# Where the sample's key-query products and the final row scaling are computed in the projection stage

## The reference, cut to what matters

```python
# sample, each of the strided branches, over the cache and the new keys
scores = jnp.einsum('bthd,btnhd->bthn', q, kg) * (dh ** -0.5)
...
mixed = jnp.concatenate([o_a, o_b, o_c], axis=-1)
y = x + mixed @ w_out
...
def rmsnorm(x, g):          # the final norm, over D_MODEL = 1024
    y = xf * lax.rsqrt(jnp.mean(xf * xf, axis=-1, keepdims=True) + RMS_EPS)
    return y * g
```

## Time and profile before

| what | us |
|---|---|
| median of three runs | 1598.43 |
| lowest, highest | 1595.06, 1598.65 |
| profiled execution, its own time | 1597.11 |
| its span, first to last instruction | 1595.4 |

### The profile page before, as it was taken

How to read it: one execution, slowest core, us unless ns; L and a number is a source line. 1 busy time by engine, 2 the same in 40 slices (tenths; PEclk the granted TensorE clock), 3 DMA queues, 4 the chain that set the end, 5 groups by cost and what they waited for, 6 DMA issues and landing times. The chain is left out here.

```text
span 1595.4 us, 40264 instructions
## 1 busy us (share of the span) xinstructions
PE 1525.6 (96%) x16281; PEld 1328.2 (83%) x16281; DVE 973.1 (61%) x2108; ACT 848.5 (53%) x1633; POOL 554.9 (35%) x664
## 2 busy tenths in 40 slices
PE   7999999999999999999999998899999889999997
PEld 6998889999898989989898987886777567777775
DVE  4437766433377878788777773336666666465642
ACT  5437777322376666778888882545777511211210
POOL 1102221200155655566565542215664411121110
PEclk9999999999999999999999999997999999999999
DMA  6310112135413122121212112559990476766641
GB/s 242 103 54 30 35 43 68 57 104 145 118 38 80 49 69 63 41 77 39 69 35 68 31 46 63 149 131 218 269 207 15 152 230 197 228 218 209 216 151 40
DMA packets 196294, 175.39 MB, mean 110 GB/s; under 512 B 84915, under 2 KB 180686, under 8 KB 193806
## 3 DMA queue, kind: packets, MB, share of 16 engines
q1 hardware_dynamic: 196110, 172.82, 37.7%
HBM read 123.18 MB, written 52.84 MB: 110 GB/s over the span
## 5 line engine op out<-in xcount | busy, mean ns | idle before, releaser
L49 PE MATMUL f_bank<-c_ht,c_whi 128*128 128x384 f32 (+1 forms) x864 | 310.3, 359 | 0.5
L50 PE MATMUL f_bank<-c_ht,c_whi 128*128 128x384 f32 (+1 forms) x864 | 301.2, 349 | 1.1 <-issue 1.1
L51 PE MATMUL f_bank<-c_ht,c_wlo 128*128 128x384 f32 (+1 forms) x864 | 301.4, 349 | 0.7 <-issue 0.7
L633 POOL TENSOR_TENSOR f_scr<-f_scr 128x192 f32<-128x192 f32 (+1 forms) x180 | 113.2, 629 | 209.8 <-PE f_tps L1294 207.5
L49 PEld LDWEIGHTS f_bank<-c_ht,c_whi 128*128 128x128 f32 x864 | 162.1, 188 | 15.7 <-DVE c_wlo L929 3.0
L50 PEld LDWEIGHTS f_bank<-c_ht,c_whi 128*128 128x128 f32 x864 | 162.2, 188 | 11.5 <-issue 2.7
L51 PEld LDWEIGHTS f_bank<-c_ht,c_wlo 128*128 128x128 f32 x864 | 162.2, 188 | 8.7
L49 PE MATMUL a_s<-a_whi,a_mhi 128*128 128x512 f32 (+1 forms) x306 | 124.7, 407 | 4.8 <-DVE a_y L2533 4.8
L50 PE MATMUL a_s<-a_wlo,a_mhi 128*128 128x512 f32 (+1 forms) x306 | 121.2, 396 | 0.0
L878 ACT ACTIVATE f_scr<-f_scr 128x384 f32<-128x384 f32 (+1 forms) x180 | 92.2, 537 | 38.7 <-POOL f_scr L634 38.4
L1088 DVE COPY_PREDICATED f_scr<-f_scr,f_tps 128x384 f32<-128x384 int32 (+1 forms) x150 | 94.5, 630 | 22.8 <-PE f_tps L1294 7.5
(11 more groups left out here) (405 smaller groups left out, 3850.4 us busy)
## 6 DMA issues: line engine op xcount, KB each, us to landing
f_wraw<-in_w_in SPq DMA_DIRECT2D x27, 512.0 KB, 4.1
zs<-f_stage SPq DMA_DIRECT2D x48, 192.0 KB, 2.4
a_k<-in_ck SPq DMA_DIRECT2D x48, 192.0 KB, 5.2
a_v<-in_cv SPq DMA_DIRECT2D x48, 192.0 KB
f_scr<-in_xp SPq DMA_DIRECT2D x16, 512.0 KB, 4.4
a_x<-in_xp SPq DMA_DIRECT2D x16, 512.0 KB, 5.4
out_y_prompt<-a_y SPq DMA_DIRECT2D x16, 512.0 KB, 3.4
zt<-f_stage SPq DMA_DIRECT2D x38, 192.0 KB, 1.8
```

What stands on the lines that cost most here:

```text
L49: nc.tensor.matmul(out, w_hi, m_hi, start=start, stop=False)
L50: nc.tensor.matmul(out, w_hi, m_lo, start=False, stop=False)
L51: return nc.tensor.matmul(out, w_lo, m_hi, start=False, stop=stop)
L633: G.tensor_tensor(d[:, :, hs:], b[:, :, hs:], r, ALU.subtract)
```

## The change

Two pieces of work change their engine; their places in the list stay. The key-query product `sr` goes from GpSimd to VectorE. The operation of `ph` on VectorE is taken apart: ScalarE multiplies the tile's rows by the row factor, and GpSimd then multiplies them by `gfin`. A new semaphore, `rowed`, stands between the two.

```diff
-                elif kind == "sr":                                  # GpSimd
-                    pool.wait_ge(Z["k_in"], BASE + KLOADS * (n + 1))
-                    read(pool, "Q", n)
-                    G.tensor_tensor(kk[:, 0:FJ, :], kk[:, 0:FJ, :], qrep[:].unsqueeze(1).to_broadcast([P, FJ, AW]),
-                                    ALU.mult).then_inc(Z["product"], 1)
+                elif kind == "ph":                                  # GpSimd
+                    p, w = n % 2, rows_of(n)
+                    if n == 0:
+                        pool.wait_ge(Z["g_in"], BASE + 16)
+                    pool.wait_ge(Z["rowed"], BASE + n + 1)
+                    G.tensor_tensor(yy[p][:w, :], yy[p][:w, :], gfin[:w, :], ALU.mult).then_inc(Z["final"], 1)
...
+                elif kind == "ph":                                  # ScalarE
+                    p, w = n % 2, rows_of(n)
+                    act.wait_ge(Z["rstd"], BASE + n + 1)
+                    A(yy[p][:w, :], yy[p][:w, :], ACT.Copy, scale=small[p][:w, 2:3]).then_inc(Z["rowed"], 1)
...
+                elif kind == "sr":                                  # VectorE
+                    dve.wait_ge(Z["k_in"], BASE + KLOADS * (n + 1))
+                    read(dve, "Q", n)
+                    V.tensor_tensor(kk[:, 0:FJ, :], kk[:, 0:FJ, :], qrep[:].unsqueeze(1).to_broadcast([P, FJ, AW]),
+                                    ALU.mult).then_inc(Z["product"], 1)
...
-                elif kind == "ph":                                  # VectorE
-                    p, w = n % 2, rows_of(n)
-                    if n == 0:
-                        dve.wait_ge(Z["g_in"], BASE + 16)
-                    dve.wait_ge(Z["rstd"], BASE + n + 1)
-                    V.scalar_tensor_tensor(out=yy[p][:w, :], in0=yy[p][:w, :], scalar=small[p][:w, 2:3], in1=gfin[:w, :],
-                                           op0=ALU.mult, op1=ALU.mult).then_inc(Z["final"], 1)
```

More of the change, by code:

```diff
@@ L1839, in attend_project @@
                                         "p_far_t", "p_near", "p_far", "o_sum", "o_row", "o_back", "out", "held", "w_hi", "w_lo",
-                                        "turned", "copied", "hi", "lo", "y_sum", "resid", "square", "mean", "rstd", "final")}
+                                        "turned", "copied", "hi", "lo", "y_sum", "resid", "square", "mean", "rstd", "rowed", "final")}
         KLOADS, VLOADS = 16 * (FJ + 1), 16 * (FJ + 2)
```

## The result

The changed kernel takes 1622.55 us (median of four runs, 1619.96 to 1624.53) where the kernel before, run beside it, takes 1597.29: a ratio of 1.0151, interval 1.0132 to 1.0169, or 25.3 us more. The direction was forecast, the size not: 1614, with an upper bound of 1621.

The account below looks back on a forecast made before the run. TensorE was taken to bound the projection, other engines counting only where it waits. Places 1.6 + 9.2, clock 4.0 and tail 2.2 sum to 17.0 us on 1597.1, giving 1614; eight-in-ten range 1604 to 1621.

Parts of the forecast that it names:

- The port: VectorE beside GpSimd: GpSimd's product of 1024 elements starts 0.37 us ahead of the split and holds it, +2.31 us.
- the case in which the casts wait: The split's casts also wait for GpSimd's product: it begins 3.54 us after the power instead of 1.23, +2.31.
- GpSimd's product and ScalarE's scaling: Output rows after the power: scaling 1.06 us, product of 1024 elements 2.28; the end is 3.54 us after the power.
- The five places: TensorE's waits for `far_rows`: b = 0 pays 1.6 us; b = 2, 4, 5 and 7 pay 2.31 each, 9.2.
- tile 0's stall: VectorE's `ph` of tile 0, slowed beside GpSimd's key product; its going shortens TensorE's 4.75 us wait by 2.7.
- The key product costs nothing: On VectorE, eight times 2.55 us, in idle stretches or in place of the stall; cost nothing.
- The tail: After the last tile's power, scaling and product end at 1592.96 instead of 1590.74: +2.2 us before the store.
- The clock: TensorE's clock falls twice more, behind b = 5's longer wait and b = 0's new one: 2.0 us each, 4.0.
- The price of 1.4 to 1.5: Work in us that TensorE loses at its lower clock after one wait: 1.5 after 4.8 us, 1.4 after 1.70.
- The bound of 9: Upper bound of the clock loss in us: each of the five waits longer by about 2; the lower bound was 0.
- More is late: Rival: groups b = 1, 3 and 6 lose their 1.1 us, or the clock stays low longer: 1620 to 1625, chance 0.08.

## Why the prediction was right and where it was wrong

- *The port.* Right. The trace of before had no cast of these forms beside a GpSimd operation; the prediction took the case in which the casts wait, and 15 first casts take 2304 ns on average for 551. This agrees with what the Trainium skill, SBUF — State Buffer, section "Who interferes with whom", says of casts. The runs show what is held and for how long; that a port holds it they don't show.
- *GpSimd's product and ScalarE's scaling.* 2.28 and 1.06 us were taken, 2.39 and 1.15 measured: the right rows were chosen, each 0.1 short. The Trainium skill, GPSIMD Engine Reference, section 3.1, gives 4497 ns for 2048 columns, half of which is 2.25, an estimate that lies 0.14 under the measured 2.39.
- *The five places.* Right: 10.8 us forecast, 10.6 measured in the waits. b = 2, 4, 5 and 7 wait 15.4 us for 6.3, where 9.2 more were forecast. At b = 0 the gain from tile 0's stall and the loss met as described.
- *The key product costs nothing.* Right at seven groups (no idle time before it, 2544 ns, alone 0.9998). At b = 0 it takes back what the lost stall would give, as was said.
- *The tail.* Right: 2.2 forecast, 2.3 measured.
- *The clock.* This step failed. 4.0 us were taken, two new falls of 2.0 each, and 11.3 were lost: the term was mis-sized by 7.3, more than the 5.9 by which the 17.0 fell short of 22.9 (the small sizes above and the 0.8 us of an earlier start go the other way). Two things were wrong in it. The new falls, at b = 0 and 5, cost 3.3 us each (half of 6.52 and of 6.70 busy us). And the three places that had a stretch already were given nothing more, while b = 2 lost 3.0 us more than before and b = 7 1.6; only b = 4 stayed as it was. The price of 1.4 to 1.5 was read behind one wait of 1.70 and one of 4.75 us (for the first the window ends ahead of the stretch, so it was 1.6). As the two were alike, nothing in them said that waits of 3.6 to 4.0 would cost more. The row that would have warned is the one at b = 4, which the prediction doesn't use: behind 1.61 us of wait it has a stretch of 6.6 us, against 3.2 at its neighbours. The bound of 9 in that part ("each of the five longer by about 2") was nearer the truth than the value chosen, and with it the sum is 22.0. But even that was too low, and the range stopped at 1621. That the waits set off most of the lost clock is shown by the runs with added matmuls; what decides the length of a single stretch stays open.
- *More is late* had this case at 0.08 and 1620 to 1625. Its second half, a clock that stays low longer, was the outcome; the waits of b = 1, 3 and 6, its first half, did not come.

What stays open besides: the profiled execution is the fastest of the changed kernel's four, and its others are up to 4.6 us longer. They have no trace, so where they spend it isn't known. In the two that are over 4 us longer the mean granted clock over the span is 0.971 and 0.972, for 0.974 in the profiled one. Over 1620 us that is 5 and 3 us of lost clock, where 4.2 and 4.6 us are to be explained: it fits, which is argued, not shown.

## What to carry to other kernels

On a kernel whose TensorE is always busy, price a wait twice: once for its length, and once for the clock behind it, which here cost about as much again over five waits (19.3 and 17.8 us), though a single wait can cost much less or more. When work is moved to GpSimd, look for casts and two-input operations on VectorE that will start under it, and for the chain that they sit in. Reordering the chain, so that what TensorE waits for is issued ahead of what it needs two steps later, was worth more than any move between engines.

## What the runs showed of the hardware

Over all runs, behind waits of 1.0 to 1.7 us TensorE ran at half clock for 0 to about 7 us, behind 2.0 to 2.9 us for 0 to about 7 as well, and behind 3.6 to 4.0 us for about 7 to 10. But the one wait of 4.75 us at tile 0 had 3.4 us behind it in the kernel before and 6.8 in the same kernel with added matmuls further on, and one fall of 3.2 us had no wait ahead of it. With dummy matmuls in the wait, 0.40 to 0.50 us of standing still left no half-clock stretch at b = 2 and 4 of the changed kernel, but 0.47 us left one of 3.4 at b = 2 of the kernel before.

A cast that began 0.39 us after a GpSimd product ended 0.42 us behind it, whether the product took 2.39 us or 1.29. A reduction of 2304 elements a partition ran beside a GpSimd product and kept its 2.54 us. GpSimd's power, begun 0.20 us ahead of a cast, took 0.80 us for 0.54, and the cast kept its 0.56.
